# Two-layer encoder trunk on one core: another order of the first loads, a dense network that begins with two column chunks of tile 0, and a last dense chunk fed by halves

## What is computed

```
for l in (0, 1):
    h = rms_norm(x, pre_mix_gain[l])
    q, k, v, u = split(h @ w_in[l])                       # 512, 128, 128, 512 columns
    y = concat(rms_norm(window_attention(q, k, v)), rms_norm(multiscale_pool(u)))
    x = x + rms_norm(y @ w_out[l], post_mix_gain[l])
    h = rms_norm(x, pre_ffn_gain[l])
    if l == 0:  f = (silu(h @ w_gate) * (h @ w_up)) @ w_down   # dense, 2816 hidden columns
    else:       f = sum of the 2 best of 8 experts, each such a network, weighted by a softmax of router logits
    x = x + rms_norm(f, post_ffn_gain[l])
```

## Time and profile before

| | |
|---|---|
| median of 3 runs | 1185.26 us (1184.65 to 1189.02) |
| profiled execution, its own time | 1186.54 us |
| its span, first to last instruction | 1184.8 us |
| PE busy / DVE busy / ACT busy | 1113.8 / 889.5 / 750.2 us |
| mean granted TensorE clock | 0.971 of full speed |
| chain that ended last, by engine | PE 88%, DVE 6%, ACT 2%, DMA 2%, issue 2% |

### The profile page before, as it was taken

The page is one execution under the profiler, slowest core; times in us unless marked ns, Lnnn a source line. Parts: engine busy times, 40 slices in busy tenths (PEclk is TensorE's granted clock), DMA queues, the critical chain, the costliest instruction groups (busy, mean ns, idle before and its releaser), DMA issues.

```text
span 1184.8 us, 13851 instructions
## 1 busy us (share of the span) xinstructions
PE 1113.8 (94%) x5410; PEld 930.2 (79%) x5410; DVE 889.5 (75%) x743; ACT 750.2 (63%) x737; POOL 38.3 (3%) x76
## 2 busy tenths in 40 slices
PE   5998999997897599999999999999999999999995
PEld 4986888886895378888888888888888888888783
DVE  4666454545467478888989888888988888888885
ACT  5555334434374167777777777777777777777764
POOL 3000000000001000000000000000000000000200
PEclk9998999998899699999999999999999999999998
DMA  8646655542423569999999999999999999999981
GB/s 284 213 151 219 207 179 197 173 162 70 169 72 125 213 249 385 379 379 393 371 373 396 372 383 385 370 391 383 372 390 381 376 386 380 381 368 374 397 313 74
DMA packets 174594, 350.65 MB, mean 296 GB/s; under 512 B 9248, under 2 KB 58416, under 8 KB 174528
## 3 DMA queue, kind: packets, MB, share of 16 engines
q1 hardware_dynamic: 169648, 332.43, 77.2%
q0 software_dynamic: 4592, 16.30, 3.9%
q10 hardware_dynamic: 288, 1.05, 0.2%
HBM read 343.97 MB, written 5.77 MB: 295 GB/s over the span
## 4 chain that ended last, share of the span: by engine, by line
PE 88%; DVE 6%; ACT 2%; DMA 2%; issue 2%; SPq 0%; DVEq 0%; ACTq 0%
PE ps L1109 27%; PE ps L1110 27%; PE ps L1111 27%; PE ps L1365 1%; DMA raw_gu<-in_w_in 1%; DVE lo_gu L1831 1%; PE ps L1116 1%; PE ps L1408 1%; PE ps L1187 1%; DVE lo_d L1838 1%; ACT hi_gu L961 0%; DVE rows L1595 0%; DMA raw_d<-in_moe_w_down 0%; PE ps L1168 0%; PE ps L1301 0%
## 5 line engine op out<-in xcount | busy, mean ns | idle before, releaser
L1831 DVE TENSOR_TENSOR lo_gu<-raw_gu,hi_gu 128x2048 fp32r<-128x2048 f32 x176 | 396.2, 2290 | 65.3 <-ACT hi_gu L961 65.3
L1109 PE MATMUL ps<-hi_gu,xt_hi 128*128 128x512 f32 (+1 forms) x1040 | 404.4, 389 | 7.2 <-DVE xt_lo L1577 4.0
L1111 PE MATMUL ps<-hi_gu,xt_lo 128*128 128x512 f32 (+1 forms) x1040 | 398.0, 383 | 0.0
L1110 PE MATMUL ps<-lo_gu,xt_hi 128*128 128x512 f32 (+1 forms) x1040 | 397.3, 382 | 0.0
L961 ACT CAST hi_gu<-raw_gu 128x2048 fp32r<-128x2048 f32 x176 | 327.8, 1909 | 11.3 <-PE ps L1111 8.3
L971 ACT CAST hi_d<-raw_d 128x1024 fp32r<-128x1024 f32 x172 | 172.2, 1050 | 132.8 <-PE ps L1111 132.8
L1109 PEld LDWEIGHTS ps<-hi_gu,xt_hi 128*128 128x128 f32 x1040 | 197.6, 190 | 45.2 <-DVE xt_lo L1577 5.2
L1111 PEld LDWEIGHTS ps<-hi_gu,xt_lo 128*128 128x128 f32 x1040 | 197.3, 190 | 38.3
L1110 PEld LDWEIGHTS ps<-lo_gu,xt_hi 128*128 128x128 f32 x1040 | 197.8, 190 | 35.6
L1838 DVE TENSOR_TENSOR lo_d<-raw_d,hi_d 128x1024 fp32r<-128x1024 f32 x172 | 202.8, 1221 | 18.3 <-ACT hi_d L971 17.7
L1109 PE MATMUL ps<-hi_d,ht_hi 128*128 128x512 f32 x432 | 172.0, 398 | 4.1 <-DVE ht_lo L1733 3.7
(11 more groups left out here) (226 smaller groups left out, 767.5 us busy)
## 6 DMA issues: line engine op xcount, KB each, us to landing
raw_gu<-in_moe_w_gate SPq DMA_DIRECT2D x176, 512.0 KB, 5.8
raw_gu<-in_moe_w_up SPq DMA_DIRECT2D x176, 512.0 KB, 7.3
raw_d<-in_moe_w_down SPq DMA_DIRECT2D x88, 1024.0 KB, 8.1
raw_gu<-in_dense_w_gate SPq DMA_DIRECT2D x22, 512.0 KB, 3.7
raw_gu<-in_dense_w_up SPq DMA_DIRECT2D x22, 512.0 KB, 4.7
raw_d<-in_dense_w_down SPq DMA_DIRECT2D x11, 1024.0 KB, 4.8
raw_gu<-in_w_in SPq DMA_DIRECT2D x16, 512.0 KB, 9.8
raw_gu<-in_w_out SPq DMA_DIRECT2D x16, 512.0 KB, 6.4
```

Of the source, the lines that this page charges most:

```text
L1109: pe.matmul(o, a_hi, b_hi, start=first, stop=False)
L1110: pe.matmul(o, a_hi, b_lo, start=False, stop=False)
L1111: return pe.matmul(o, a_lo, b_hi, start=False, stop=last)
L1831: dve.tensor_tensor(flat_piece(lo_gu, slot_at), flat_piece(raw_gu, slot_at), flat_piece(hi_gu, slot_at).bitcast(F32), ALU.subtract).then_i ...
```

## The change

**First loads.** ACT loads tile 0 of x only; SP loads tile 1 of x between `M_KV` and `M_U0`. POOL issues the first gain's load ahead of all constants, the sinks' load after the masks, and waits for the third `hi` piece (`gu_hi_done` 3, which is `M_Q0`) before it issues the next gains and `pool_w`. ACT and DVE normalise tile 1 after tile 0's splits, and PE turns tile 1's rows after `kv(l, 0)`.

**Begin of the dense network.** The new `begin` replaces the first two steps. The order of gate and up is chunk 0 tile 0, chunk 1 tile 0, chunk 0 tile 1, chunk 1 tile 1 (`FIRST_HIDDEN`, whose third number is the place in `silu` and `hidden`). Tile 1's rows are turned inside chunk 1 of tile 0, after six of its eight k. The last piece, `split_first(l, 3)`, moves ahead of `transposed(l, T_FFN, 1)` and `low_part(l, T_FFN, 1)`, in both layers.

**End of the dense network.** The last chunk's hidden rows are turned in the middle of `down` of the chunk before, into buffers of their own (`ht_hi_end`, `ht_lo_end`), and the last down weights are split by halves, the first as soon as the half of `hi_d` has been read (`d_half_used`). ACT loads the table of the square root there, ahead of `M_Q0`.

```diff
+        dense_end = ExitStack()
+        ht_hi_end = sb("ht_hi_end", [P, 2, S], F32R, at=dense_end)
+        ht_lo_end = sb("ht_lo_end", [P, 2, S], F32R, at=dense_end)
+        dense_end.close()
         probs0 = sb("probs0", [P, N_HEADS, P], at=mix)
...
-        def ffn_steps(eng, step, tail):
-
-            for c in (0, 1):
-                step(c, use_ffn(0) + c, c)
+        def ffn_steps(eng, begin, step, tail):
+
+            begin()
             with eng.Fori(0, (NCH - 3) // 2) as m:
                 for c in (2, 3):
                     step(c, m * 2 + (use_ffn(0) + c), m * 2 + c, m)
...
+        FIRST_HIDDEN = [(0, 0, 1), (1, 0, 0), (0, 1, 1), (1, 1, 1)]
 
...
-            for m in range(2 * MIX_USES):
+            load_mix(0, M_KV)
+            sp.dma_start(x_res[:, 1, :], x[0, P:2 * P, :]).then_inc(x_loaded[1], 16)
+            for m in range(M_U0, 2 * MIX_USES):
                 load_mix(0, m)
...
-            pool.memset(ident[:], 0.0).then_inc(const_made, 1)
-            pool.memset(eps[:], EPS).then_inc(const_made, 1)
-            pool.wait_ge(const_made, 2)
-            pool.affine_select(out=ident[:], in_=ident[:], compare_op=ALU.not_equal, fill=1.0, base=0,
-                               pattern=[[-1, P]], channel_multiplier=1).then_inc(const_made, 1)
...
-            pool.dma_start(sinks[:].rearrange("p l h -> p (l h)"),
-                           attn_sinks.rearrange("(a l) h -> a (l h)", a=1).broadcast_to([P, DEPTH * N_HEADS])
-                           ).then_inc(sinks_loaded, 16)
...
             load_gain(0)
+            pool.memset(ident[:], 0.0).then_inc(const_made, 1)
+            pool.memset(eps[:], EPS).then_inc(const_made, 1)
+            pool.wait_ge(const_made, 2)
...
+            pool.dma_start(sinks[:].rearrange("p l h -> p (l h)"),
+                           attn_sinks.rearrange("(a l) h -> a (l h)", a=1).broadcast_to([P, DEPTH * N_HEADS])
+                           ).then_inc(sinks_loaded, 16)
+
+            pool.wait_ge(gu_hi_done, 3)
             for n in (1, 2):
                 load_gain(n)
             pool.dma_start(pool_w_sb[:], pool_w[0].rearrange("g c d -> c g d")).then_inc(pool_w_loaded, 16)
...
-            for t in range(TT):
-                act.dma_start(x_res[:, t, :], x[0, t * P:(t + 1) * P, :]).then_inc(x_loaded[t], 16)
+            act.dma_start(x_res[:, 0, :], x[0, 0:P, :]).then_inc(x_loaded[0], 16)
...
             def mixing(l):
                 if l == 0:
                     act.activation(spare[:, 1:2], eps[:, 0:1], ACT.Sqrt)
-                    for t in range(TT):
-                        pre_mix(l, t)
+                    pre_mix(l, 0)
                     split_mix(l, M_KV)
                     transposed(l, T_MIX, 0)
+                    pre_mix(l, 1)
                     split_mix(l, M_U0)
                     transposed(l, T_MIX, 1)
                     split_mix(l, M_Q0)
...
                 pre_ffn(l, 1)
+                if l == 0:
+                    first_silu(0)
+                split_first(l, 3)
                 transposed(l, T_FFN, 1)
-                split_first(l, 3)
+
+            def first_silu(idx):
+                chunk, t, place = FIRST_HIDDEN[idx]
+                act.wait_ge((gu_tile0, gu_used)[t], chunk + 1)
+                if idx >= 2:
+                    act.wait_ge(h_done, (1, 3)[idx - 2])
+                act.activation(silu[:, place, :], ps[:, B_GU + idx % 2, 0:FC], ACT.Silu).then_inc(silu_done, 1)
...
-                def turn(chunk):
+                def turn(chunk, to=ht_hi):
                     act.wait_ge(h_turned, chunk + 1)
-                    act.copy(ht_hi[:], ps[:, B_TP, :].rearrange("p (k s) -> p k s", k=2)).then_inc(ht_hi_done, 1)
+                    act.copy(to[:], ps[:, B_TP, :].rearrange("p (k s) -> p k s", k=2)).then_inc(ht_hi_done, 1)
+
+                def begin():
+                    use = use_ffn(0) + 2
+                    first_silu(1)
+                    split_d(0, None)
+                    first_silu(2)
+                    split_gu(2, use, use % 2, 0, 32 * (use // 2 + 1))
+                    turn(0)
+                    split_gu(2, use, use % 2, 1, 32 * (use // 2 + 1))
+                    first_silu(3)
...
                 def tail(chunk):
-                    split_d(NCH - 1, None)
-                    turn(chunk)
-
-                ffn_steps(act, step, tail)
+                    act.wait_ge(d_loaded[chunk % 2], 16 * (chunk // 2 + 1))
+                    for k in range(2):
+                        act.wait_ge(*((d_half_used, 1) if k == 0 else (d_used, chunk)))
+                        act.copy(hi_d[:, k, :], raw_d[:, chunk % 2, k, :]).then_inc(d_hi_done, 1)
+                        if k == 0:
+                            turn(chunk, ht_hi_end)
+                    act.activation(spare[:, 1:2], eps[:, 0:1], ACT.Sqrt)
...
             def mixing(l):
                 turn_rows(l, T_MIX, 0)
-                turn_rows(l, T_MIX, 1)
+                if l:
+                    turn_rows(l, T_MIX, 1)
                 xt_ready(l, T_MIX, 0)
                 pe.wait_ge(gu_lo_done, mix_count(l, M_KV))
                 kv(l, 0)
+                if not l:
+                    turn_rows(l, T_MIX, 1)
                 pe.wait_ge(gu_lo_done, mix_count(l, M_U0))
                 u(l, 0, 0)
...
+                def gate_up(use, parity, chunk, t, before_second, idx=None):
...
-                        if isinstance(chunk, int) and chunk == 0 and t == 1 and k == 0:
+                        if isinstance(chunk, int) and (chunk, t, k) == (1, 0, 6):
                             turn_rows(0, T_FFN, 1)
-                            xt_ready(0, T_FFN, 1)
                         a = slice(t * P, (t + 1) * P)
-                        last = mm3(ps[:, B_GU + t, :], xt_hi[:, k, a], xt_lo[:, k, a], hi_gu[:, parity, k, :],
+                        last = mm3(ps[:, B_GU + (idx % 2 if isinstance(idx, int) else t), :], xt_hi[:, k, a], xt_lo[:, k, a], hi_gu[:, parity, k, :],
...
-                def down(c, chunk):
+                def down(c, chunk, between=None):
                     pe.wait_ge(ht_lo_done, chunk + 1)
                     ended = c == NCH - 1
+                    hi, lo = (ht_hi_end, ht_lo_end) if ended else (ht_hi, ht_lo)
...
                             cols = slice(n * 512, (n + 1) * 512)
-                            last = mm3(ps[:, B_Y + 2 * t + n, :], ht_hi[:, k, a], ht_lo[:, k, a],
+                            last = mm3(ps[:, B_Y + 2 * t + n, :], hi[:, k, a], lo[:, k, a],
                                        hi_d[:, k, cols], lo_d[:, k, cols], c == 0 and k == 0, ended and k == 1)
                         if ended and (t, k) == (0, 1):
                             last.then_inc(ffn_tile0, 1)
+                        if between and (t, k) == (1, 0):
+                            last.then_inc(d_half_used, 1)
+                            between()
                     last.then_inc(d_used, 1)
...
+                def turn_first(t):
+
+                    pe.wait_ge(h_done, 1 + 2 * t)
+                    for k in range(2):
+                        c0 = k * TT * P + t * P
+                        last = pe.transpose(ps[:, B_TP, c0:c0 + P], hidden[:, 1, k * P:(k + 1) * P], ident[:])
+                    if t:
+                        last.then_inc(h_turned, 1)
+
+                def begin():
+                    use = use_ffn(0)
+                    hook = (None, None, lambda: turn_first(0), lambda: turn_first(1))
+                    for idx, (chunk, t, _) in enumerate(FIRST_HIDDEN):
+                        if idx == 2:
+                            xt_ready(0, T_FFN, 1)
+                        gate_up(use + chunk, (use + chunk) % 2, chunk, t, hook[idx] or (lambda: None), idx)
+                    down(0, 0)
...
+                    gate_up(use, (use_ffn(0) + c) % 2, chunk, 0, lambda: turn(chunk - 1))
                     gate_up(use, (use_ffn(0) + c) % 2, chunk, 1, lambda: None)
-                    if c:
-                        down(c - 1, chunk - 1)
+                    down(c - 1, chunk - 1, (lambda: turn(chunk)) if c == NCH - 1 else None)
 
                 def tail(chunk):
-                    turn(chunk)
                     down(NCH - 1, chunk)
...
                 if l == 0:
-                    for t in range(TT):
-                        pre_norm(l, PRE_MIX, t)
+                    pre_norm(l, PRE_MIX, 0)
                     split_mix(l, M_KV)
                     low_part(l, T_MIX, 0)
+                    pre_norm(l, PRE_MIX, 1)
                     split_mix(l, M_U0)
                     low_part(l, T_MIX, 1)
                     split_mix(l, M_Q0)
...
                 pre_norm(l, PRE_FFN, 1)
+                if l == 0:
+                    first_hidden(0)
+                split_first(l, 3)
                 low_part(l, T_FFN, 1)
-                split_first(l, 3)
+
+            def first_hidden(idx):
+                place = FIRST_HIDDEN[idx][2]
+                dve.wait_ge(silu_done, idx + 1)
```

(21 more changed lines are left out.)

42 lines of the change are left out of this document (20 added, 22 removed).

## The result

The changed kernel takes 1174.84 us in the median of four runs (1173.94 to 1176.87), the kernel before 1187.14 (1184.65 to 1189.35) in four. The medians lie 12.3 us, or 1.0%, apart. The ratio of the runs is 0.9904, with a 95% interval of 0.9886 to 0.9922; the quotient of the medians, 0.9896, lies in it. The profiled execution took 1173.94 by its own time. Its span is 12.6 shorter than the one before.

The account below looks back on a forecast made before the run. PE was taken to bound the kernel (88% of the chain), with gains left in four late-starting places. 3.4 + 2.7 + 5.2 + 2.8 = 14.1 off 1185.3 gave 1171.2 us, range 1168.3 to 1177.0.

Parts of the forecast that it names:

- A: Start: gain and first weights land sooner, PE's first product at 13.45 us; gains 3.4 us, bounds 1.9 and 4.5.
- C: First dense chunk: the new order shortens PE's waits and part of the clock's loss; gains 2.7 us, bounds 0.8 and 4.0.
- D: End of the dense network: the reciprocal starts at 288.4 instead of 293.63; gains 5.2 us.
- E: Ahead of layer 1's router: cast and lo move off the path to its products; gains 2.8 us, or 1.4.
- 2.0 MB at 0.38 ... land at 8.0: Start: x tile 0, gain and M_KV at 0.38 MB per us from about 2.5 us on land at 8.0.
- The wait of 0.70: Start: PE's wait for the next piece at 22.94 us goes, a gain of 0.7 us.
- the waits of 2.0, 2.4 and 1.0: First dense chunk: PE's new gaps in the new order, of 2.0, 2.4 and 1.0 us.
- I take half of the old loss: First dense chunk: half the old clock loss of 2.5 us stays in the new gaps, 1.3 off a gain of 4.0.
- From it to the transposes at 300.47 nothing changes: End of the dense network: from the reciprocal to the transposes the time stays as before, so 5.2 us are gained.
- The experts passed all on: Rival on the experts: bound by DMA, they take back what is gained; no change, 1185 us; chance 0.05.
- Gaps move only: Rival: the first dense chunk gives 0.8, the end 4, the router 1.4, the start 2; 8 us, 1177; chance 0.10.

Follow-up runs that it names:

- gain_late: The changed kernel with POOL's order alone undone (constants and the sinks' load ahead of the first gain's load): 1178.04 us.
- no_end_halves: The changed kernel with the end of the dense network undone (hidden rows turned ahead of the last down, its weights split in one piece): 1177.10 us.
- no_two_chunks: The changed kernel with the first dense chunk undone (chunk 0 for both tiles, then chunk 1): 1175.12 us.
- busy_all: The changed kernel with PE's long waits outside the experts filled with transposes of the identity that nobody reads: 1164.17 us.
- x1_on_act: The changed kernel with tile 1 of x loaded from ACT's queue again, right behind tile 0: 1175.54 us.
- busy_layer1: The changed kernel with 55 unread transposes of the identity on PE between layer 0's end and the wait for layer 1's first rows: 1171.35 us.
- no_router_order: The changed kernel with layer 1's last piece of expert 0's weights split behind tile 1's xt parts again: 1175.58 us.

## Why the prediction was right, and where it was not

The forecast of 1171.2 is 3.6 below the median, inside the range, and faster as said. Half of the distance is the drop, 12.3 instead of 14.1 (12.6 in the profiled execution). The other half is the kernel before, whose median is 1187.14 over four runs and was 1185.26 over the three shown. In part the sum is right by luck: by the landmarks the four terms came to 14.8, and a loss of 2.2 that the prediction has nowhere brings them to 12.5.

| term | forecast | by the landmarks | with the clock held |
|---|---|---|---|
| A, start | 3.4 | 2.96 | not tried |
| C, first dense chunk | 2.7 | 3.65 | 0.1 |
| D, end of the network | 5.2 | 5.28 | 2.9 |
| clock at the start of layer 1 | none | -2.24 | none |
| E, router | 2.8 | 2.87 | 2.9 |

The landmarks are: for A the stop behind chunk 0 tile 0; for C the first cast of the down weights of chunk 1, 129.42 before and 122.81 after, less A; for D the reciprocal, 11.89, less A and C; for the clock ACT's first copy of `k_rows` (307.98 to 298.33, 9.65, against 11.89); for E the router products (12.55) less 9.68 at the transposes before them. The rows of C and of the clock, before and after:

```profile
129.42 2.01 ACT L921 CAST hi_d<-raw_d 128x1024 fp32r<-128x1024 f32 x2 [5.11 <-PE ps L1111]
...
307.98 0.37 ACT L790 COPY k_rows<-ps 128x256 f32<-128x256 f32 x1 [1.77 <-PE ps L1111]
```

```profile
122.81 2.01 ACT L939 CAST hi_d<-raw_d 128x1024 fp32r<-128x1024 f32 x2 [5.11 <-PE ps L1142]
...
298.33 0.37 ACT L799 COPY k_rows<-ps 128x256 f32<-128x256 f32 x1 [4.01 <-PE ps L1142]
```

**A.** The chain was right: gain, rows, transposes, then `M_KV`, its cast and `lo`, `xt_lo`. The step that failed is "2.0 MB at 0.38 ... land at 8.0": `M_KV` landed at 9.36. In gain_late, with the gain's packets behind, it lands at 7.66. The forecast took one rate for all bytes; in the trace the gain's long packets take most of the bytes beside the weights' short ones (0.44 of 0.61 MB from 6 to 8 us). The first product was forecast at 13.45 and came at 14.77. The wait of 0.70 went, and the clock rose 3.3 behind the first product, as before (3.4), so nothing was lost to it. That is no rule: with the same order of loads it rose 2.7 behind it in no_end_halves and 4.7 in no_two_chunks. That the total was still near 3.4 is two errors against each other. What A is worth alone isn't settled: undone in the changed kernel it cost 5.0 at the stop behind chunk 0 tile 0.

**C.** Tile 1 started 11.9 us behind the stop, forecast 11.8, and the waits of 2.0, 2.4 and 1.0 came as 1.86, 0.49 and 0.98. The clock fell just behind the first of the three, at 96.6, and was back at 100.0. The first half's slow matmuls lay in time that PE would have waited for the second half of the weights anyway: where they ran at 1.00, in busy_all, that wait was 2.12 instead of 0.49. The step "I take half of the old loss" was too dear: of 4.0 only 0.35 was lost, not 1.3. With the clock held the order is worth 0.1: nearly all that it gained is the low clock of the old, longer gap. The Trainium skill (TensorE: Matmul & The Clock Gate, HAM oscillation) warns of gaps longer than these. By its rule the clock holds in all three; the trace doesn't agree, with 0.50 from 96.6 on, 1.0 us behind a wait of 1.86. But in x1_on_act the same wait, 1.83 long, was passed at 1.00, so the length of the gap alone doesn't decide it in these traces.

**D.** From the last `down` but one to the reciprocal 6.8 us were measured, 7 forecast, and DVE's piece for `M_Q0` sets the end, as written. The step that failed is the sentence "From it to the transposes at 300.47 nothing changes", which is true, but the sum ends there. The old last `down` at the low clock was counted as a gain, and the clock that then rises later, 5.1 us behind the first product of layer 1, wasn't counted as a loss. no_end_halves shows the one and busy_layer1 the other.

**E.** Right in mechanism and size.

**Rivals.** The experts passed all on: 12.57 at their first product, 12.6 at their end. Not every pair of traces does so: no_two_chunks is 1.9 late at their first product and 1.0 at PE's end. "Gaps move only" was right of the first dense chunk with the clock held, and nowhere else.

## What to carry to other kernels

Where an engine's clock depends on what it did before, a wait has two prices, its own length and that of the slow work behind it. Take both from the trace, and follow the clock past the place of the edit. Parts undone one by one needn't add up: here they gave 6.0 of 12.3 in the medians. With the clock held the landmarks (0.1, 2.9, 2.9) and the medians (-0.2, 3.1, 2.7) of three parts agree within 0.3. And idle time of PE that can't be removed can be filled: 284 useless transposes are worth 10.7 us here, nearly as much as the whole change (12.3).

## What the runs showed of the hardware

In the changed kernel the gain's load, issued on POOL's queue at 1.35 us, sent none of its packets by 4 us and 19 by 6 us, while the loads issued on SP's and ACT's at 0.82 had moved 0.54 MB by 4 us. In the kernel before and in gain_late, where that queue's first load is issued at 1.86, it sent none by 6 us. Queues in flight together share by packets and not by bytes, as above. Transposes that nobody reads keep the granted clock at 1.00: in busy_layer1 it holds through 55 of them from 282.0 to 288.2, where it fell at 284.4 without them. And the runs of one kernel differ by up to 5.8 us (no_router_order). That the clock falls and rises at other places from run to run is the likely cause: the two fastest of these runs show a mean clock of 0.977, the other four 0.974 to 0.976. It wasn't tried apart.
